# Stick-breaking attention in steps of 128 keys for two heads at once, with the query and key projections between the steps

## The reference

```
z = (q @ k.T) / 8                                # 512 queries x 512 keys
causal = key position < query position
log_1m = where(causal, log_sigmoid(-z), 0)       # = -softplus(z)
excl   = cumsum from the last key down(log_1m) - log_1m
a      = where(causal, exp(log_sigmoid(z) + excl), 0)
out    = a @ v
```

## Time and profile before

| | us |
|---|---|
| median of the timed runs | 2349.79 |
| the profiled execution, its own time | 2367.59 |
| its span, first to last instruction | 2365.7 |
| TensorE busy | 2284.6 (97%) |
| VectorE, ScalarE, GpSimd busy | 1269.8, 852.1, 321.8 |

### The profile page before, as it was taken

One profiled execution on the slowest core, in us unless ns is written; L12 is line 12 of the kernel. 1 busy time (PEld: TensorE's weight loads), 2 busy tenths in 40 slices (PEclk: granted clock), 3 DMA queues, 4 the chain that ended last, 5 costly groups with the idle time before them and its releaser, 6 DMA issues. The chain is left out here.

```text
span 2365.7 us, 28730 instructions
## 1 busy us (share of the span) xinstructions
PE 2284.6 (97%) x11284; PEld 1808.6 (76%) x11284; DVE 1269.8 (54%) x1982; ACT 852.1 (36%) x1394; POOL 321.8 (14%) x320
## 2 busy tenths in 40 slices
PE   8899999999999999999999999999999999999998
PEld 7678778768888887875568888888785558888887
DVE  5766555354444445337645545555547884555454
ACT  4433554233222224136643222224234663222223
POOL 1301340000000003003311000001034551000001
PEclk9999999999999999998899999999998999999999
DMA  5233124313333332320013333333220003233331
GB/s 158 72 107 90 35 63 151 89 45 90 98 98 98 91 96 80 98 80 1 1 36 92 96 98 98 97 91 111 89 89 19 2 2 89 92 96 98 98 93 50
DMA packets 292661, 188.08 MB, mean 80 GB/s; under 512 B 7856, under 2 KB 286640, under 8 KB 292528
## 3 DMA queue, kind: packets, MB, share of 16 engines
q1 hardware_dynamic: 292240, 186.05, 26.3%
q10 hardware_dynamic: 288, 0.21, 0.0%
HBM read 184.14 MB, written 2.10 MB: 79 GB/s over the span
## 5 line engine op out<-in xcount | busy, mean ns | idle before, releaser
L466 DVE TENSOR_TENSOR wl<-raw,wh 128x1024 fp32r<-128x1024 f32 x336 | 414.3, 1233 | 750.4 <-ACT wh L456 750.3
L470 PE MATMUL ps<-xb_x,wh 128*128 128x512 f32 (+1 forms) x2000 | 620.8, 392 | 0.0
L456 ACT CAST wh<-raw 128x1024 fp32r<-128x1024 f32 x336 | 348.9, 1039 | 743.6 <-PE ps L470 728.3
L470 PEld LDWEIGHTS ps<-xb_x,wh 128*128 128x128 f32 (+1 forms) x2000 | 373.9, 187 | 79.8
L470 PE MATMUL ps<-xb_x,wl 128*128 128x512 f32 (+1 forms) x1000 | 392.1, 392 | 0.0
L470 PE MATMUL ps<-XH,wh 128*128 128x512 f32 x680 | 271.5, 399 | 9.1 <-issue 3.6
L470 PE MATMUL ps<-XH,wl 128*128 128x512 f32 x680 | 267.5, 393 | 0.0
L470 PE MATMUL ps<-XL,wh 128*128 128x512 f32 x680 | 267.3, 393 | 0.0
L560 POOL TENSOR_TENSOR acc<-acc,sq 128x512 f32<-128x512 f32 x55 | 76.1, 1383 | 1338.2 <-ACT sq L547 1336.8
L470 PEld LDWEIGHTS ps<-xb_x,wl 128*128 128x128 f32 (+1 forms) x1000 | 187.2, 187 | 44.5
L470 PEld LDWEIGHTS ps<-XH,wh 128*128 128x128 f32 x680 | 129.5, 190 | 39.6 <-issue 8.6
(11 more groups left out here) (340 smaller groups left out, 3490.4 us busy)
## 6 DMA issues: line engine op xcount, KB each, us to landing
raw<-in_mlp_w SPq DMA_DIRECT2D x128, 512.0 KB, 3.8
raw<-in_w_gate_up SPq DMA_DIRECT2D x44, 512.0 KB, 3.7
raw<-in_w_in SPq DMA_DIRECT2D x29, 512.0 KB, 3.6
raw<-in_sb_w_qkv SPq DMA_DIRECT2D x24, 512.0 KB, 3.6
raw<-in_w_down SPq DMA_DIRECT2D x22, 512.0 KB, 3.3
raw<-in_w_out_mix SPq DMA_DIRECT2D x16, 512.0 KB, 4.0
raw<-in_w_kv SPq DMA_DIRECT2D x16, 512.0 KB, 3.7
raw<-in_nsa_w_kv SPq DMA_DIRECT2D x12, 512.0 KB, 3.5
```

Source lines behind the costliest of these rows:

```text
L456: e.copy(shaped(WH[i % NH], i), shaped(RAW[i % NR], i)).then_inc(*w_hi.up(i))
L466: e.tensor_tensor(shaped(WL[i % NH], i), shaped(RAW[i % NR], i), shaped(WH[i % NH], i).bitcast(F), ALU.subtract).then_inc(*w_lo.up(i))
L470: return e.matmul(out, a, b, start=start, stop=stop, skip_group_check=True)
```

## The change

The heads are worked in 32 steps instead of 16. Step n is the block j of 128 keys (in the order 3, 2, 1, 0) of the heads 2c and 2c+1 together. Each head of a pair has its own bank of the three bank pairs PS[0..5]; one bank, PS[6], holds the outputs; NB takes the query and key projections of the next pair, of which one half (12 of 24 matmuls) is issued in each step. Only the projections sq0 and sq8 stand ahead of the values now, and the list of weight units follows. The mask is added with the scores, before the absolute value, so the 0/1 multiplication on VectorE is gone. The absolute value is now a bitwise operation of VectorE, and all exp and ln are ScalarE's. The outputs go to a pair XO that lies where queries and keys lie; the feed-forward layer behind the stage now reads X instead of XB; the norm "one" has its own tile rs1.

```diff
-    for o in range(16):
+    for o in (0, 8):
         unit(f"sq{o}", wcols(sbq, 128 * o))
...
+    for c in range(1, 8):
+        for o in (c, 8 + c):
+            unit(f"sq{o}", wcols(sbq, 128 * o))
...
+    ST = [(c, j) for c in range(8) for j in (3, 2, 1, 0)]
+    NST = len(ST)
+    Lp = Ring([Buf(ph.sb(f"L{i}", [128, 2, 512])) for i in range(4)])
...
+    def parts(n):
+
+        return [slice(0, 1), slice(1, 2)] if ST[n][1] < 2 else [slice(0, 2)]
...
+    def next_qk(n):
+
+        u, half = (n + 1) // 2 + 2, (n + 1) % 2
+        return (u if u < 16 else None), half
...
+            if u is not None and half == 0:
+                plan(NB, ("sqk", QK[u]), (v_made, ("sqk", QK[u])))
...
+            for m in range(2):
+                plan(PS[2 * at + m], ("sk", n, m), (a_made, ("sw", n, m)))
+            plan(Lp.next(), ("L", n), (mixed, ("so", n)))
...
+            if j == 3:
+                plan(PS[6], ("so", c), (x_lo, ("so", c)))
...
+        for m in range(2):
+            p0 = 64 * m
+            mm(e, bk[m], k_s[p0:p0 + 64, c, 128 * j:128 * j + 128], q_s[p0:p0 + 64, c, 128 * j:512], True, False)
+        for m in range(2):
+            mm(e, bk[m][:, 0:128], Ib[:, :], maskb[:, 2, :], False, False).then_inc(*scored.up("z", n, m))
...
+        for m in range(2):
+            h = 2 * c + m
+            f = mm(e, o[64 * m:64 * m + 64, 128 * j:512], v_s[:, j, 64 * h:64 * h + 64], L[:, m, 0:wd[j]], j == 3,
+                   j == 0)
...
+        pe_stick_qk(e, -1)
+        for n in range(NST + 3):
+            if n < NST:
+                pe_stick_scores(e, n)
+            if 2 <= n < NST + 2:
+                pe_stick_cum(e, n - 2)
+            pe_stick_qk(e, n)
+            if n >= 3:
+                pe_stick_out(e, n - 3)
...
+            project(e, f"so{o}", XO, "so", t[:, :], ("soo", o))
...
+        for n in range(-1, NST + 3):
+            if 2 <= n < NST + 2:
+                weights_of(n - 2)
+            u, half = next_qk(n)
+            if u is not None and half == 0:
+                act_weights(e, UI[f"sq{QK[u]}"] + 2)
...
+                    e.activation(L[:, part, 0:wd[j]], L[:, part, 0:wd[j]], ACT.Exp, scale=-1.0).then_inc(
+                        *a_made.up("exp", n, part.start))
...
+                    e.activation(L[:, part, 0:wd[j]], L[:, part, 0:wd[j]], ACT.Ln, bias=ONE1).then_inc(
+                        *a_made.up("ln", n, part.start))
...
+            e.tensor_scalar(L[:, m, 0:w].bitcast(I32), got(("sk", n, m))[:, 0:w].bitcast(I32), 0x7FFFFFFF, None,
+                            ALU.bitwise_and).then_inc(*v_made.up("abs", n, m))
...
+        for n in range(-1, NST + 3):
+            u, half = next_qk(n)
+            if u is not None and half:
+                dve_weights(e, UI[f"sq{QK[u]}"] + 2)
+            if half == 0 and 2 < (n + 1) // 2 + 2 <= 16:
+                dve_stick_qk(e, QK[(n + 1) // 2 + 1])
+            if 0 <= n < NST:
+                dve_stick_abs(e, n)
+            if 1 <= n < NST + 1:
+                dve_stick_lo(e, n - 1)
+            if 0 <= n < NST:
+                dve_stick_terms(e, n)
...
-    fm = Ffn("m", [4] * 8, "m", PH0 + 8 * S * 8, "st", [(g_made, ("fe", 7))])
+    fm = Ffn("m", [4] * 8, "m", X, PH0 + 8 * S * 8, "st", [(g_made, ("fe", 7))])
```

More of the change, by code:

```diff
@@ L1680, in pe @@
                 else:
[L1681 removed]
+                    project(e, self.units[n], self.x, self.norm_tag(), t[:, :], key)
                 if n == 0:
@@ L1841, in plan_stick @@
         plan_spread("one")
[L1842 to L1852, removed]
+        pairs = Ring([0, 1, 2])
+        for n in range(-1, NST):
+            u, half = next_qk(n)
+            if u is not None and half == 0:
+                plan(NB, ("sqk", QK[u]), (v_made, ("sqk", QK[u])))
+            if n < 0:
+                continue
+            c, j = ST[n]
+            at = pairs.next()
+            for m in range(2):
+                plan(PS[2 * at + m], ("sk", n, m), (a_made, ("sw", n, m)))
+            plan(Lp.next(), ("L", n), (mixed, ("so", n)))
+            last = 4 * c + 3
+            plan(Lh[j].next(), ("Lh", n), (scored, ("cum", last)))
+            plan(Ll[j].next(), ("Ll", n), (scored, ("cum", last)))
+            if j == 3:
+                plan(PS[6], ("so", c), (x_lo, ("so", c)))
         for o in range(8):
@@ L1860, in pe_stick_scores @@
+    def pe_stick_scores(e, n):
+        c, j = ST[n]
         e.wait_ge(*v_made.at("sqk", c))
         e.wait_ge(*v_made.at("sqk", 8 + c))
[L1862 to L1888, removed]
-        e.wait_ge(*a_made.at("tok", "sv1", 3))
[L1890 to L1893, removed]
+        bk = [take(e, ("sk", n, m))[:, 0:wd[j]] for m in range(2)]
@@ new lines, in pe_stick_scores, with pe_stick_cum @@
+        for m in range(2):
[3 more added lines that the diff above has]
+            mm(e, bk[m][:, 0:128], Ib[:, :], maskb[:, 2, :], False, False).then_inc(*scored.up("z", n, m))
+    def pe_stick_cum(e, n):
+        c, j = ST[n]
+        for part in parts(n):
+            e.wait_ge(*v_made.at("lo", n, part.start))
+            for m in heads_of(part):
+                t = got(("sk", n, m))
+                for i in range(j, 4):
+                    hb, lb = got(("Lh", 4 * c + 3 - i)), got(("Ll", 4 * c + 3 - i))
+                    out = t[:, 128 * (i - j):wd[j]]
+                    by = trir[:, 0 if i == j else 1, :]
+                    mm(e, out, by, hb[:, m, :], False, False)
+                    f = mm(e, out, by, lb[:, m, :], False, i == 3)
+                f.then_inc(*(scored.up("cum", n) if m else scored.up("cum0", n)))
@@ L1939, in act_stick @@
             act_tokens(e, f"sv{blk}", lambda t: v_s[:, t, 512 * blk:512 * blk + 512], 512, 4, inv("st"))
-        act_rs(e, "one", [(v_made, ("sqk", 15))])
+        e.wait_ge(*mixed.at("spread", "one"))
+        e.copy(rs1[:, :], got(("spread", "one"))[:, :]).then_inc(*a_made.up("rs", "one"))
         e.preload_act_table_set("natural_log_exp_and_others")
[L1943 to L1961, removed]
+        def weights_of(n):
+            L, j = got(("L", n)), ST[n][1]
+            for m in range(2):
+                e.wait_ge(*scored.at("cum" if m else "cum0", n))
+                e.activation(L[:, m, 0:wd[j]], got(("sk", n, m))[:, 0:wd[j]], ACT.Exp).then_inc(*a_made.up("sw", n, m))
@@ new lines, in dve_stick @@
+        for n, o in enumerate(QK[0:2]):
+            dve_weights(e, UI[f"sq{o}"] + 2)
+        s = got(("sum", "st"))[:, 0:8].rearrange("p (i c) -> p c i", c=2)
+        e.wait_ge(*a_made.at("root", "one"))
+        e.reciprocal(inv("one"), std("one")).then_inc(*v_made.up("inv", "one"))
+        e.wait_ge(*v_made.at("inv", "one"))
+        e.tensor_tensor(std("one"), s[:, 1, :], inv("one"), ALU.mult).then_inc(*v_made.up())
+        e.wait_ge(*v_made.now())
+        e.tensor_tensor(std("one"), std("one"), inv("one"), ALU.mult).then_inc(*v_made.up("root", "st"))
@@ L2052, in dve_stick @@
+        e.wait_ge(*a_made.at("root2", "st"))
+        e.reciprocal(inv("st"), std("st")).then_inc(*v_made.up())
+        e.wait_ge(*v_made.now())
+        e.tensor_tensor(inv("st"), inv("st"), inv("one"), ALU.mult).then_inc(*v_made.up("inv", "st"))
+        dve_diag(e, "st")
+        dve_weights(e, UI["sv00"] + 2)
+        for o in QK[0:2]:
+            dve_stick_qk(e, o)
         for blk in range(2):
```

247 lines of the change are left out of this document (104 added, 143 removed).

## The result

The changed kernel takes 2313.01 us (median of 4 runs, 2312.22 to 2313.40), the kernel before in the same comparison 2351.68 (4 runs, 2348.63 to 2354.00). The ratio is 0.984 [0.982, 0.985]: 38.7 us faster, inside the predicted range (2282 to 2320), where the forecast was 2295 and a gain of 54.8. The forecast's own range was 2284 to 2310 and does not hold the result; the wider one does. The profiled execution of the changed kernel took 2313.40 us, span 2311.5. One of the 17 executions of the kernel before that ran beside the second set of experiments took 3718.24 us at a mean granted clock of 0.56 and is in none of the ratios.

What follows compares the result with a forecast made beforehand. TensorE was taken to bound the stage: work 171.0, waits 6, start 0.6, end 6.1 and clock 1.7 give 185.4 against 240.2 us. That is 54.8 off the median 2349.8, so 2295, range 2282 to 2320.

Steps and rivals of the forecast that it cites:

- the clock falls as often as now: Rival for the heads: half clock stays as frequent, 20.6 us more than forecast, 2316; chance 0.12.
- The two signs for the overlap: Heads' scores: both start less than 0.02 us apart, and masks follow 1.06 us later for 512 columns.
- Scores and values of a pair cost as one head's: TensorE in the heads: two heads' adjacent float32 matmuls overlap; 11.85 us a pair, 31.0 saved over eight.
- The rival without overlap: Heads: the two heads' matmuls do not overlap, giving back 31.0 us, 2326; chance 0.05.
- The projections stay at 5.44: The 14 projections moved between the steps keep their 5.44 us each, 76.2 in all.
- A change of tiling mode: Steps of the heads: 48 added mode changes, if twice as dear as 0.1 us, cost some 5 us more.
- Steady steps wait 6: Steady steps: contention beside GpSimd's product makes TensorE wait 6 us in all, between 0 and 15.
- The slack of 1.5: Steady steps: TensorE's 9.4 us of other work covers the 7.9 us chain to Ll, leaving 1.5.
- Start 0.6, end 6.1: TensorE idle time: 0.6 us at the start waiting for NB, 6.1 at the uncovered end, between 3 and 12.
- One fall of the clock, at the end: Heads: a single fall to half clock, 1.7 us, bounded by none and 22.3.
- The bitwise |z| at 0.68: VectorE's absolute value out of PSUM: taken at 0.68 us, no time either way, 0 to 8 if the chain lengthens.
- Its distance to the median, 17.8, lies outside this stage and stays: Profiled execution against median, kernel before: 17.8 us placed outside the stage, so the whole 54.8 came off the median 2349.8.

Runs made afterwards that it cites:

- the heads set apart: Changed kernel with a mask matmul between the two heads' scores and their values issued apart, so never next to each other: 2360.82 us, ratio 1.000.
- The filler's run: Kernel before, with three bfloat16 matmuls of 512 columns, results never read, put in TensorE's wait before each head's scores from the third on: 2349.29 us, ratio 0.996.
- the one with all projections ahead: Changed kernel with all 16 projections ahead of the values again and none between the steps: 2332.80 us, ratio 0.988.

## Why the prediction was right, and where it was not

The direction and the mechanism held, and so did the sum of the stage. The point forecast was 18 us too low. That the stated range holds 2313 is luck: the forecast's own waits and bounds reach only to 2310, and the range was widened to 2320 for a rival (the clock falls as often as now, 2316) that did not come true. The two signs for the overlap came as named: the scores of the two heads start less than 0.02 us apart (both at 1041.13), and 1.06 us lie between them and the masks. By the prediction's own steps:

- **Scores and values of a pair cost as one head's.** Right: scores of four widths 2.96 a pair (forecast 2.96), values 2.76 (2.75), cum 5.63 (5.66), masks 0.37 (0.48). The rival without overlap is settled by the heads set apart.
- **The projections stay at 5.44.** Mis-sized: a half takes 2.88 to 2.90, not 2.72, since each of the 28 halves pays for its way into and out of a group. 28 times 0.18 is 5 us. The prediction had counted such a price (0.15 to 0.20) for scores and values and left it out here.
- **A change of tiling mode.** The groups of scores and values cost what the entry and exit times of the earlier trace rows gave, so the changes are not twice as dear there; the halves cost 5 us more. The Trainium skill (TensorEngine Tiling (Array Packing), Key Properties) says that a change of mode drains the engine; a projection half between two other groups is 0.18 longer than half of an undivided row of projections, which agrees with a drain of about that size. The prediction left its own estimate for this, also 5 us, out of the sum; but that was for 48 added changes at 0.1 more each, not for 28 halves at 0.18, and that the two come to the same is chance. No run here separates the drain from the rest of a group's entry.
- **Steady steps wait 6.** They wait 0 up to step 27. The slack of 1.5 held although VectorE works beside GpSimd's products; the lengthened subtraction of the earlier trace rows shows here too, with a longest Ll of 1.79 us against a median of 0.61, but never on the path.
- **Start 0.6, end 6.1.** 0.68, and 4.0 from step 27 on.
- **One fall of the clock, at the end.** One, of 1.7 us. The rival with as many falls as before is out: the steady stretch is at 1.00. The filler's run, and the one with all projections ahead, where waits come back and the clock is at 0.95, point to the missing waits as the reason.
- **The bitwise |z| at 0.68.** At most 0.69 (512 columns), at least 0.27 (128), by the row of L2031; the second row is the subtraction for Ll named above:

```profile
L2031 DVE TENSOR_SCALAR st_L<-ps x64: 271/487/692, 983.6 to 1151.2; 128x128 int32<-128x128 int32 x16, 128x256 int32<-128x256 int32 x16, 128x384 int32<-128x384 int32 x16, 128x512 int32<-128x512 int32 x16
L2047 DVE TENSOR_TENSOR st_Ll<-st_L,st_Lh x48: 409/614/1785, 987.9 to 1155.7; 128x512 fp32r<-128x512 f32 x24, 128x384 fp32r<-128x384 f32 x16, 128x256 fp32r<-128x256 f32 x8
```

- **"Its distance to the median, 17.8, lies outside this stage and stays".** This is the step that failed, and nearly the whole error. The distance was half clock in the heads: the profiled execution of before had 22.3 us of it, the one at 2348.65 had 126.8 - 125.8 = 1.0. The median run of before is near the second, so it never had most of the clock that the sum took away; taken out of the gain, the distance leaves 54.8 - 17.8 = 37.0, against 38.7 measured. The numbers to see it stood in the view of the stretches: a clock of 0.85 in the heads, and a profiled execution 17.8 us over the median that had to lose them somewhere. The sum for the stage came out right (185.4 against 183.0) partly by luck: the waits that never came (6 and 2) made up for the projection halves (5).

On the clock: the rows show it at 0.83 behind waits of 0.69 in one execution and at 1.00 behind the same waits in another, and at 1.00 once 0.63 us of matmuls (8.49 - 7.86) fill them. The Trainium skill (TensorE: Matmul & The Clock Gate, "Why this matters for your kernels") warns of pauses between bursts of matmuls only when they are long. Here no pause in the later heads of the profiled executions is longer than 0.69 us, and the slowest execution still took 27 us more than the kernel with the filler (2376.24 against 2349.29), so on this point the measurement decides.

## What to carry to other kernels

When a profiled execution lies above the median of the runs, find the stretch with the low clock first and take that distance out of the gain before forecasting the median; a loss by clock that the change removes is worth only what the median run has of it. Half-array matmuls of two heads pay only when they are issued directly one behind the other: a single mask matmul between the two heads' scores cost the whole overlap there. Dense work cut into small pieces and laid between dependent steps is cover, and its worth is the idle time and the clock falls it prevents; count about 0.15 to 0.2 us for each piece, as measured here, and look at the bank it uses.

## What the hardware showed that was not expected

- The same program on the same chip loses its clock in some executions and not in others: in the first set 18 of 35 at 2348 to 2353.5 us, 15 at 2366 to 2376, with mean clocks of 0.985 to 0.989 and 0.975 to 0.981. Twelve executions with 0.63 us more of TensorE's work per head were all within 3.2 us. The two profiled executions show no difference between their later heads but the clock: the waits of 0.69 us and their releaser are the same.
- Two float32 score matmuls of 512 columns on the two halves of the rows take 1.06 us together and 1.06 us each; both timelines are shown above. The overlap is complete.
